# VectorE branches right behind the selection; diagonals and slot numbers behind the first rows' copy; six small loads on ScalarE's queue

## The chip, the cores and the metric

The kernel runs on one core of a Trainium2 chip. The metric is the device time of one execution in microseconds (us): the median of 3 runs of the kernel before is 1742.47 us (1740.42 to 1742.9).

## The reference, cut to what matters

The program is a small network of 256 tokens of width 1024, in float32: a pooling mixer, a mixture of experts (layer 0), latent attention, a mixture of experts (layer 1), and then a second block (state space scan, linear attention, cross attention, feed-forward). The change touches both mixtures of experts, and in them only the routing and the start of the loop over the experts:

```python
def hier_moe(h, rg_w, rg_b, re_w, re_b, w_gate, w_up, w_down):
    gp = softmax(ht @ rg_w + rg_b)                 # 4 groups: top 1
    el = (ht @ re_w + re_b) of the chosen group    # 8 experts: top 2
    gates = g_prob[:, None] * top_p / top_p.sum(-1, keepdims=True)
    expert_ids = g_idx[:, None] * 8 + top_i        # 32 experts, 256 x 2 assignments
    # assignments are sorted by expert, every expert does
    y = (silu(xr @ w_gate[e]) * (xr @ w_up[e])) @ w_down[e]
    # and row y is added to its token, times its gate
```

## The kernel before, in words

Every engine has one program in order of its instructions; semaphores order them against each other. SyncE's queue (SP) loads nearly all weights as slabs of 2 MB into a ring of six places; one further slab per layer goes to a place of its own in the arena (`load_ahead`). A slab may be loaded when the one that held its place is done, which TensorE (PE) tells by `slabs_done`. Each of the 32 experts has three slabs: w_gate, w_up, w_down.

At the start of a mixture of experts PE computes the router's logits, VectorE (DVE) the top group, the top two experts of each token, the number of tokens of each expert (`cnt`), their running sum (`incl`) and from them the sorted position of each assignment (`pos`). The first position of each expert and the largest count go to `starts` (L1868, L1869, semaphore `route_done`). DVE then writes the selection matrix `sel` in two halves (L1875 to L1884). PE sorts the tokens with it (`sort`, L804): `sort(0)` fills the first half of the sorted rows in PSUM; DVE (`sorted_out`, L1904, k tiles 0 to 3) and ScalarE (ACT, L1481, k tiles 4 to 7) copy it to `xs` in SBUF. PE has a piece of the cross attention's keys behind `sort(0)` (L941 to L944).

Behind the selection DVE before writes eight diagonal tiles (L1886 to L1890: positions and gates as diagonals, from which PE's L823 makes rows by a matmul with ones) and the slot numbers of the gates (L1891 to L1896, and in layer 0 a reciprocal for another stage, L1899, for which GpSimd, POOL, waits). Then each of DVE, ACT and PE reads the largest count into a register (L1978, L1543, L946) and branches (L1980, L1545, L948) to one of two bodies, with one window of 64 rows per expert or with four. On this data it is the one with one window, `experts(1)`. 

DVE's body loads two start positions into registers (L1964), copies half 0 out of PSUM, waits until ACT has too, and copies the rows of the first expert and then of the second into two window buffers (`window`, L1925, copy L1933). PE's first matmuls of the experts (`gate_up`, L847, matmul L863) wait for the first window. After `gate_up` of expert 0 PE does the first `beside` (L817): the diagonals' matmul (L823, waits for the second `select_ready`) and half of `sort(1)`; then `gate_up` of expert 1, the other half of `sort(1)`, and then `turn_hid` of expert 0 (L873, transposes L879). This one waits for `hidden`, which needs ACT's `silus` (L1490, L1496) and DVE's product (L1940), and for `slots_ready`, DVE's copy of the diagonals' rows (L1943), which stands behind that product.

SP, in layer 0, waits behind the seven slabs that fit ahead of the experts for `route_max`, and then issues the four router loads of layer 1 (`router_loads`, L531 to L534) and the two halves of `b_in` (L547), all of small pieces; behind them stands the slab that takes the first place that comes free (L574). ACT issues its own transfers on its own queue, among them `kx_park` (L1446), and in `experts` of layer 0 runs on to `silus` of expert 0 right behind it (L1531, L1539).

Of the kernel before, what the change touches and what calls it, by code (L numbers as in the profile page):

```python
# [21 lines left out]
ALU = mybir.AluOpType  # L22
# [3 lines left out]
P = 128  # L26
T = 256
TT = T // P
# [23 lines left out]
TOP_K = 2  # L52
# [264 lines left out]
def program(nc, a, out):  # L317
    with ExitStack() as ctx:
# [24 lines left out]
        def cc(name):  # L343
            at, n = CONST_COLS[name]
            return const[:, at:at + n]
# [161 lines left out]
        gain2 = ar(7680, D)  # L507

        block = ctx.enter_context(nc.Block())


        @block.sync
        def _(sp):
# [15 lines left out]

            def router_loads(layer):  # L530
                sp.dma_start(rw[:, :, 0:GROUPS], a["router_group_w"][layer].rearrange("(k p) g -> p k g", p=P)).then_inc(s["row_loaded"], 16)  # L531
                sp.dma_start(rw[:, :, GROUPS:], a["router_expert_w"][layer].rearrange("(k p) g -> p k g", p=P)).then_inc(s["row_loaded"], 16)
                sp.dma_start(rb[:, 0:GROUPS], a["router_group_b"][layer].partition_broadcast(P)).then_inc(s["row_loaded"], 16)
                sp.dma_start(rb[:, GROUPS:], a["router_expert_b"][layer].partition_broadcast(P)).then_inc(s["row_loaded"], 16)  # L534

            sp.dma_start(memt, a["mem_2"].rearrange("b (t p) d -> p (b t) d", p=P)).then_inc(s["mem_loaded"], 16)
            router_loads(0)

            sp.wait_ge(s["vec2_loaded"], 16 * (len(VEC_PARTS) - FIRST_VECTORS))
            sp.wait_ge(s["pool_loaded"], 16 * 3)  # L540

            def loads_ahead():

                sp.wait_ge(s["route_max"], 1)
                router_loads(1)
                for ri, n in enumerate(("re", "im")):
                    sp.dma_start(b_in[:, ri], a[f"s5_b_{n}_2"][0].rearrange("(j g) p h -> (g p) j h", g=2)).then_inc(s["s5_loaded"], 16)  # L547

# [13 lines left out]
            def experts(layer, n0):  # L562
# [30 lines left out]
                if layer == 0:  # L593
                    load_ahead()
                    loads_ahead()
                for j in range(first + 1, 2 * RING):
# [792 lines left out]
        def _(act):  # L1389
# [61 lines left out]
            def moe(layer, name, n0):  # L1451
# [35 lines left out]
                def experts(windows):  # L1487
# [38 lines left out]
                    if layer == 0:  # L1526
                        act.wait_ge(s["xkv_mm"], 1)
                        park_keys(0, 2, 7)
                        act.wait_ge(s["slabs_done"], n0)
                        act.activation(xk_out[0][:, 2, :], PS[:, 6, 0:T], ACT.Copy).then_inc(s["xkv_out"], 1)  # L1530
                        store_keys(0, 3, 2)  # L1531
                    else:
                        act.wait_ge(s["slabs_done"], n0)
                        act.activation(xk_out[5][:, 1:3, :].rearrange("p f n -> p (f n)"), PS[:, 7, :], ACT.Copy).then_inc(s["xkv_out"], 1)
                        store_keys(5, 3, 10)
# [215 lines left out]
        def _(dve):  # L1751
# [55 lines left out]
            def moe(layer, name, n0):  # L1807
# [77 lines left out]

                for i, v in enumerate((pos, gat)):  # L1886
                    for k in range(TOP_K):
                        for t in range(TT):
                            last = dve.tensor_scalar(diag[:, i, k * TT + t, :], ident, v[:, k, t, :], None, ALU.mult)
                last.then_inc(s["select_ready"], 1)  # L1890
                for w in range(WINDOWS):  # L1891
                    dve.tensor_scalar(slot_of[:, w, :], incl, cc("row_1")[:, w:w + 1], None, ALU.add)
                    last = dve.tensor_scalar(slot_valid[:, w, :], cnt, cc("row")[:, w:w + 1], None, ALU.is_gt)
                step(last)
                step(dve.tensor_tensor(slot_of, slot_of, slot_valid, ALU.mult))
                step(dve.tensor_scalar(slot_of, slot_of, 1.0, None, ALU.subtract))  # L1896
                if layer == 0:
                    dve.wait_ge(s["s5_th"], 2)
                    dve.reciprocal(den, den).then_inc(s["s5_small"], 1)  # L1899
                dve.wait_ge(s["fgain_loaded"], 16)  # L1900
# [12 lines left out]

                dve.wait_ge(s["route_done"], q + 1)

                def experts(windows):
# [8 lines left out]
                    def window(e, w, start=None):  # L1925

                        if isinstance(e[0], int) and linear(e, windows, w) == 2:
                            sorted_wait(1)
                        if isinstance(e[0], int) and linear(e, 1, 0) >= EXPERTS:
                            return  # L1930
                        if start is None:
                            start = load_start(e)
                        dve.tensor_copy(xw[(e[1] * windows + w) % 2], xs[:, :, bass.ds(start + w * WINDOW, WINDOW)])\  # L1933
                           .then_inc(g["window"], 1)

# [27 lines left out]

                    second = after((0, 0), 0)  # L1964
                    start_0, start_1 = load_start((0, 0)), load_start(second[0])
                    sorted_out(0)
                    dve.wait_ge(s["pad_ready"], q + 1)
                    sorted_wait(0)
                    window((0, 0), 0, start_0)
                    window(*second, start_1)  # L1970
                    for w in range(windows):
# [528 lines left out]
```

## Time and profile before

| | us |
|---|---|
| median of 3 runs | 1742.47 (1740.42 to 1742.9) |
| the profiled execution, as timed | 1745.04 |
| its span in the trace | 1743.2 |
| PE busy in the span | 1630.2 (94%) |
| DVE busy | 451.9 (26%) |
| ACT busy | 232.0 (13%) |
| weights on SP's queue | 502.05 MB, 71.9% of 16 engines' span |

Times in the trace count from the start of the span. "Busy" of an engine leaves out registers, branches, semaphores and the issue of DMAs; these appear under an engine's name with a q (DVEq, ACTq, SPq), the duration of a DMA's line being what its issue took, not the transfer. In square brackets stands how long the engine sat idle before a line, and what released it. "x64" counts records; a float32 matmul has two. "PEclk" is the granted share of TensorE's 2.4 GHz clock (1.00 is 2.4 GHz, 0.50 is 1.2 GHz). "DMA share" is the mean busy share of the 16 DMA engines.

### The profile page before, as it was taken

The numbers are of one execution on the slowest core, as the hardware profiler recorded it, in microseconds if no ns is written. First come the engines' busy times: TensorE is split into PE (matmuls) and PEld (weight loads), VectorE is DVE, ScalarE is ACT, GpSimd is POOL, SyncE is SP. The second block draws the span as 40 slices with busy tenths as digits, with TensorE's granted clock in tenths as the row PEclk, the third lists the DMA queues.
The fourth block names the chain that finished last, engine by engine and source line by source line (L and its number), as shares of the span: only waits on it lengthen the run. The fifth ranks groups of instructions, "written<-read, shape, count | busy, mean of one in ns | idle before, by whom it ended". The sixth has DMA issues, their size and how long they took to land.

```text
span 1743.2 us, 22328 instructions
## 1 busy us (share of the span) xinstructions
PE 1630.2 (94%) x9157; PEld 1014.8 (58%) x9157; DVE 451.9 (26%) x967; ACT 232.0 (13%) x503; POOL 97.5 (6%) x165
## 2 busy tenths in 40 slices
PE   7999988888899999999988888889999998999998
PEld 7755444444446657655444444448577777688843
DVE  4211111111113324221111111134976211244411
ACT  4110100000002121111000000021123012100000
POOL 2200000000000000193000000010000000000000
PEclk9999999999999999999999999998999999999999
DMA  9999999999997342899999999995233541444400
GB/s 334 350 378 426 427 427 425 426 425 426 426 413 279 136 169 98 318 417 425 427 425 426 427 427 427 425 376 204 102 140 111 184 134 60 131 163 153 145 24 24
DMA packets 106755, 508.21 MB, mean 292 GB/s; under 512 B 16874, under 2 KB 46155, under 8 KB 73675
## 3 DMA queue, kind: packets, MB, share of 16 engines
q1 hardware_dynamic: 104411, 502.05, 71.9%
q10 hardware_dynamic: 2288, 5.40, 0.8%
q8 instruction: 37, 0.61, 0.1%
q14 instruction: 19, 0.16, 0.0%
HBM read 504.28 MB, written 3.15 MB: 291 GB/s over the span
## 4 chain that ended last, share of the span: by engine, by line
PE 39%; DMA 16%; DVE 3%; ACT 1%; issue 1%; DVEq 0%; ACTq 0%
DMA ring<-in_w_up 16%; PE PS L1355 9%; PE PS L863 6%; PE PS L1120 5%; PE PS L1365 4%; PE PS L1131 2%; PE PS L906 2%; PE PS L1294 2%; PE PS L1304 2%; PE PS L1283 2%; PE PS L892 1%; ACT XN L1412 1%; PE PS L808 0%; DVE arena L2122 0%; PE PS L1332 0%
## 5 line engine op out<-in xcount | busy, mean ns | idle before, releaser
L863 PE MATMUL PS<-ring,arena 128*64 128x256 f32 x4032 | 461.0, 383 | 69.3 <-DMA ring<-in_w_up 51.5
L863 PEld LDWEIGHTS PS<-ring,arena 128*64 128x64 f32 x4032 | 290.9, 137 | 260.5 <-DMA ring<-in_w_up 71.1
L906 PE MATMUL PS<-ring,arena 128*64 128x512 f32 x1024 | 233.8, 598 | 1.2 <-ACT arena L1504 1.2
L1940 DVE TENSOR_TENSOR arena<-PS,arena 128x256 f32<-128x256 f32 x64 | 27.2, 425 | 737.8 <-ACT arena L1496 737.8
L906 PEld LDWEIGHTS PS<-ring,arena 128*64 128x64 f32 x1024 | 68.2, 136 | 157.9 <-issue 157.9
L1355 PE MATMUL PS<-hT,ring 128*128 128x256 f32 x704 | 152.2, 379 | 0.6 <-issue 0.6
L1355 PEld LDWEIGHTS PS<-hT,ring 128*128 128x128 f32 x704 | 133.7, 190 | 18.9 <-issue 0.8
L892 PE MATMUL PS<-arena,hT 64*128 64x512 f32 x512 | 127.2, 615 | 1.9 <-ACT arena L1513 1.9
L1120 PE MATMUL PS<-hT,ring 128*128 128x256 f32 x448 | 101.1, 387 | 1.0 <-issue 1.0
L1120 PEld LDWEIGHTS PS<-hT,ring 128*128 128x128 f32 x448 | 86.6, 195 | 14.8 <-issue 2.8
L1504 ACT ACTIVATE arena<-PS 128x256 f32<-128x256 f32 x64 | 24.6, 384 | 519.3 <-PE PS L879 519.3
L1513 ACT ACTIVATE arena<-PS 128x512 f32<-128x512 f32 x64 | 38.2, 597 | 306.2 <-PE PS L906 306.2
L1365 PE MATMUL PS<-ring,arena 128*128 128x512 f32 x176 | 75.7, 592 | 0.0
L892 PEld LDWEIGHTS PS<-arena,hT 64*128 64x128 f32 x512 | 44.0, 186 | 41.5 <-issue 30.2
L1365 PEld LDWEIGHTS PS<-ring,arena 128*128 128x128 f32 x176 | 33.4, 190 | 41.7 <-issue 41.4
L1952 DVE SCALAR_TENSOR_TENSOR hT<-hT,arena 128x512 f32<-128x512 f32 x64 | 51.4, 803 | 0.2
L2117 DVE TENSOR_SCALAR arena<-PS,VT 128x256 f32<-128x256 f32 x52 | 24.9, 537 | 93.7 <-PE PS L1355 93.2
L2122 DVE SCALAR_TENSOR_TENSOR arena<-PS,VT,arena 128x255 f32<-128x255 f32 (+2 forms) x112 | 46.8, 475 | 1.2
L1412 ACT ACTIVATE XN<-X 128x1024 f32<-128x1024 f32 x18 | 18.9, 1050 | 174.7 <-DVE X L2296 72.7
L728 PE MATMUL PS<-const 128*128 128x128 f32 x222 | 29.1, 287 | 6.7 <-DMA const<-in_const 6.7
L1933 DVE COPY arena<-arena 128x512 f32 x64 | 28.2, 443 | 26.5 <-issue 23.0
L879 PEld LDWEIGHTS PS<-const,arena 128*128 128x128 f32 x128 | 20.3, 206 | 24.8 <-issue 24.7
(387 smaller groups left out, 1390.7 us busy)
## 6 DMA issues: line engine op xcount, KB each, us to landing
ring<-in_w_up SPq DMA_DIRECT2D x64, 2048.0 KB, 25.6
ring<-in_w_down SPq DMA_DIRECT2D x64, 2048.0 KB, 24.6
ring<-in_w_gate SPq DMA_DIRECT2D x62, 2048.0 KB, 25.5
ring<-in_f_w_up SPq DMA_DIRECT2D x22, 1024.0 KB, 6.6
ring<-in_w_in SPq DMA_DIRECT2D x9, 2048.0 KB, 13.2
ring<-in_f_w_down SPq DMA_DIRECT2D x5, 2048.0 KB, 7.9
arena<-in_w_gate SPq DMA_DIRECT2D x2, 2048.0 KB, 22.4
ring<-in_x_wkv SPq DMA_DIRECT2D x2, 2048.0 KB, 8.0
```

What stands on the lines that cost most here:

```text
L863: mm = pe.matmul(PS[half * WINDOW:(half + 1) * WINDOW, bank, m * half_f:(m + 1) * half_f], xw[bank][:, k, :], mat[:, k, half * half_f:(hal ...
L892: mm = pe.matmul(PS[:, 4 + 2 * t + half, :], buf[rows, t * P:(t + 1) * P], y2[rows, :], start=first, stop=last, skip_group_check=True)
L906: mm = pe.matmul(PS[half * WINDOW:(half + 1) * WINDOW, 3, :], hidT[:, w, k * WINDOW:(k + 1) * WINDOW], mat[:, k, half * 512:(half + 1) * 5 ...
L1120: mm = pe.matmul(PS[:, b, f % 2 * T:(f % 2 + 1) * T], w[:, k, f * P:(f + 1) * P], x[:, k, :], start=(k == 0), stop=(k == kx - 1))
L1131: mm = pe.matmul(PS[:, bank + t, :], x[:, k, t * P:(t + 1) * P], w[:, k, :], start=(k == 0), stop=(k == kx - 1))
L1283: mm = pe.matmul(PS[:, 2 * half + t, :], hT[:, k, t * P:(t + 1) * P], w[:, k, :], start=(k == 0), stop=(k == KD - 1))
L1355: mm = pe.matmul(PS[:, 2 * (j % 2) + h, f * T:(f + 1) * T], w[:, k, h, f * P:(f + 1) * P], hT[:, k, :], start=(k == 0), stop=(k == KD - 1))
L1365: mm = pe.matmul(PS[:, 4 + 2 * t + half, :], gF[:, c, t * P:(t + 1) * P], w[:, c - 4 * j, half * 512:(half + 1) * 512], start=(c == 0), st ...
L1412: act.activation(XN[:, t, :], src[:, t, :], ACT.Square, accum_out=ssq[:, t:t + 1]).then_inc(s["norm_ssq"], 1)
L1513: act.activation(y2, PS[:, 3, :], ACT.Copy).then_inc(g["y_sbuf"], 1)
L1952: dve.scalar_tensor_tensor(gates2, slots[:, 0, :], slot_of[:, w, bass.ds(linear(e, 1, 0), 1)], slots[:, 1, :], ALU.is_equal, ALU.mult).the ...
L2122: ins = dve.scalar_tensor_tensor(v, ps(f)[:, 0:T - back], taps[f][back], v, ALU.mult, ALU.add)
```

## The change

Three edits. (1) On DVE, the diagonals and the slot numbers are made into two functions (`spread`, `window_slots`), and called inside both bodies behind the branch: the first window's copy, `spread`, the second window's copy, `window_slots`. (2) The first window's start is the constant 0 and not a register; the second's is loaded where its window is copied. (3) SP no longer waits for `route_max` nor issues the router loads of layer 1 and `b_in`; ACT issues these six, in layer 0, behind `kx_park`'s store and before `silus` of expert 0.

```diff
--- before.py
+++ after.py
@@ -506,6 +506,12 @@
         cacc = [ar(5632 + 1024 * i, 4, T) for i in range(2)]
         gain2 = ar(7680, D)
 
+        def router_loads(eng, layer):
+            eng.dma_start(rw[:, :, 0:GROUPS], a["router_group_w"][layer].rearrange("(k p) g -> p k g", p=P)).then_inc(s["row_loaded"], 16)
+            eng.dma_start(rw[:, :, GROUPS:], a["router_expert_w"][layer].rearrange("(k p) g -> p k g", p=P)).then_inc(s["row_loaded"], 16)
+            eng.dma_start(rb[:, 0:GROUPS], a["router_group_b"][layer].partition_broadcast(P)).then_inc(s["row_loaded"], 16)
+            eng.dma_start(rb[:, GROUPS:], a["router_expert_b"][layer].partition_broadcast(P)).then_inc(s["row_loaded"], 16)
+
         block = ctx.enter_context(nc.Block())
 
 
@@ -527,24 +533,11 @@
                 sp.dma_start(s5_rows[at:at + S5J, :], a[name][0].rearrange("(j g) p -> j (g p)", g=2)).then_inc(s["s5_loaded"], 16)
             sp.dma_start(ldt2[32:32 + S5J, :], a["s5_log_dt_2"][0].rearrange("(j g) -> j g", g=2)).then_inc(s["s5_loaded"], 16)
 
-            def router_loads(layer):
-                sp.dma_start(rw[:, :, 0:GROUPS], a["router_group_w"][layer].rearrange("(k p) g -> p k g", p=P)).then_inc(s["row_loaded"], 16)
-                sp.dma_start(rw[:, :, GROUPS:], a["router_expert_w"][layer].rearrange("(k p) g -> p k g", p=P)).then_inc(s["row_loaded"], 16)
-                sp.dma_start(rb[:, 0:GROUPS], a["router_group_b"][layer].partition_broadcast(P)).then_inc(s["row_loaded"], 16)
-                sp.dma_start(rb[:, GROUPS:], a["router_expert_b"][layer].partition_broadcast(P)).then_inc(s["row_loaded"], 16)
-
             sp.dma_start(memt, a["mem_2"].rearrange("b (t p) d -> p (b t) d", p=P)).then_inc(s["mem_loaded"], 16)
-            router_loads(0)
+            router_loads(sp, 0)
 
             sp.wait_ge(s["vec2_loaded"], 16 * (len(VEC_PARTS) - FIRST_VECTORS))
             sp.wait_ge(s["pool_loaded"], 16 * 3)
-
-            def loads_ahead():
-
-                sp.wait_ge(s["route_max"], 1)
-                router_loads(1)
-                for ri, n in enumerate(("re", "im")):
-                    sp.dma_start(b_in[:, ri], a[f"s5_b_{n}_2"][0].rearrange("(j g) p h -> (g p) j h", g=2)).then_inc(s["s5_loaded"], 16)
 
             def place_free(n):
                 m = held_before(n)
@@ -592,7 +585,6 @@
                     placed(j)
                 if layer == 0:
                     load_ahead()
-                    loads_ahead()
                 for j in range(first + 1, 2 * RING):
                     placed(j)
                 turns = EXPERT_SLABS // RING
@@ -1529,6 +1521,11 @@
                         act.wait_ge(s["slabs_done"], n0)
                         act.activation(xk_out[0][:, 2, :], PS[:, 6, 0:T], ACT.Copy).then_inc(s["xkv_out"], 1)
                         store_keys(0, 3, 2)
+                        act.wait_ge(s["logits"], 1)
+                        act.wait_ge(s["route_max"], 1)
+                        router_loads(act, 1)
+                        for ri, n in enumerate(("re", "im")):
+                            act.dma_start(b_in[:, ri], a[f"s5_b_{n}_2"][0].rearrange("(j g) p h -> (g p) j h", g=2)).then_inc(s["s5_loaded"], 16)
                     else:
                         act.wait_ge(s["slabs_done"], n0)
                         act.activation(xk_out[5][:, 1:3, :].rearrange("p f n -> p (f n)"), PS[:, 7, :], ACT.Copy).then_inc(s["xkv_out"], 1)
@@ -1883,20 +1880,27 @@
                     if half == 0:
                         last.then_inc(s["select_ready"], 1)
 
-                for i, v in enumerate((pos, gat)):
-                    for k in range(TOP_K):
-                        for t in range(TT):
-                            last = dve.tensor_scalar(diag[:, i, k * TT + t, :], ident, v[:, k, t, :], None, ALU.mult)
-                last.then_inc(s["select_ready"], 1)
-                for w in range(WINDOWS):
-                    dve.tensor_scalar(slot_of[:, w, :], incl, cc("row_1")[:, w:w + 1], None, ALU.add)
-                    last = dve.tensor_scalar(slot_valid[:, w, :], cnt, cc("row")[:, w:w + 1], None, ALU.is_gt)
-                step(last)
-                step(dve.tensor_tensor(slot_of, slot_of, slot_valid, ALU.mult))
-                step(dve.tensor_scalar(slot_of, slot_of, 1.0, None, ALU.subtract))
-                if layer == 0:
-                    dve.wait_ge(s["s5_th"], 2)
-                    dve.reciprocal(den, den).then_inc(s["s5_small"], 1)
+                def spread():
+
+                    for i, v in enumerate((pos, gat)):
+                        for k in range(TOP_K):
+                            for t in range(TT):
+                                last = dve.tensor_scalar(diag[:, i, k * TT + t, :], ident, v[:, k, t, :], None, ALU.mult)
+                    last.then_inc(s["select_ready"], 1)
+
+                def window_slots(step):
+
+                    for w in range(WINDOWS):
+                        dve.tensor_scalar(slot_of[:, w, :], incl, cc("row_1")[:, w:w + 1], None, ALU.add)
+                        last = dve.tensor_scalar(slot_valid[:, w, :], cnt, cc("row")[:, w:w + 1], None, ALU.is_gt)
+                    step(last)
+                    step(dve.tensor_tensor(slot_of, slot_of, slot_valid, ALU.mult))
+                    step(dve.tensor_scalar(slot_of, slot_of, 1.0, None, ALU.subtract))
+                    if layer == 0:
+                        dve.wait_ge(s["s5_th"], 2)
+                        dve.reciprocal(den, den).then_inc(s["s5_small"], 1)
+
+                at_branch = steps[0]
                 dve.wait_ge(s["fgain_loaded"], 16)
                 if layer:
                     dve.wait_ge(s["xkv_stored1"], 16 * 2)
@@ -1912,6 +1916,8 @@
                     dve.wait_ge(s["sorted_act"], KD // 2 * (2 * q + half + 1))
 
                 dve.wait_ge(s["route_done"], q + 1)
+
+                step_dve = step
 
                 def experts(windows):
                     g = loop[layer]
@@ -1930,8 +1936,11 @@
                             return
                         if start is None:
                             start = load_start(e)
-                        dve.tensor_copy(xw[(e[1] * windows + w) % 2], xs[:, :, bass.ds(start + w * WINDOW, WINDOW)])\
-                           .then_inc(g["window"], 1)
+                        if isinstance(start, int):
+                            rows = slice(start + w * WINDOW, start + (w + 1) * WINDOW)
+                        else:
+                            rows = bass.ds(start + w * WINDOW, WINDOW)
+                        dve.tensor_copy(xw[(e[1] * windows + w) % 2], xs[:, :, rows]).then_inc(g["window"], 1)
 
                     def hids(e, w):
                         dve.wait_ge(g["silu"], linear(e, windows, w + 1))
@@ -1961,13 +1970,17 @@
                                 window(*after(next_expert(e), w))
                             window_gates(e, w)
 
-                    second = after((0, 0), 0)
-                    start_0, start_1 = load_start((0, 0)), load_start(second[0])
+                    steps[0] = at_branch
                     sorted_out(0)
                     dve.wait_ge(s["pad_ready"], q + 1)
                     sorted_wait(0)
-                    window((0, 0), 0, start_0)
-                    window(*second, start_1)
+                    window((0, 0), 0, 0)
+                    spread()
+                    if windows == 1:
+                        window((0, 1), 0)
+                    else:
+                        window((0, 0), 1, 0)
+                    window_slots(step_dve)
                     for w in range(windows):
                         hids((0, 0), w)
                         if w:
```

## Rows read from the trace of the kernel before

**Rows 1.** Timeline of PE, layer 0, start of the experts: start, duration, us.

```profile
53.56 4.48 PE L706 MATMUL PS<-arena,ring 128*128 128x256 f32 x20
60.86 8.81 PE L863 MATMUL PS<-ring,arena 128*64 128x256 f32 x64 [2.82 <-DVE arena L1933]
...
75.30 7.13 PE L863 MATMUL PS<-ring,arena 128*64 128x256 f32 x64
...
86.41 0.39 PE L879 MATMUL PS<-const,arena 128*128 128x128 f32 x2
```

**Rows 2.** Timeline of PE, layer 1, the same place.

```profile
700.13 8.58 PE L863 MATMUL PS<-ring,arena 128*64 128x256 f32 x64 [3.67 <-DVE arena L1933]
```

**Rows 3.** Stretches: us, PE, PEld, DVE, ACT, POOL, PEclk, DMA share, GB/s.

```profile
61.40:64.80 3.40, 3.40 (x20) 2.38 (x18) 0.00 (x0) 0.00 (x0) 0.11 (x1) 0.50 0.78 81
...
1450.00:1460.00 10.00, 6.88 (x40) 5.91 (x39) 6.45 (x8) 3.10 (x9) 0.00 (x0) 1.00 0.37 120
```

**Rows 4.** Stretches in layer 0's loop over the experts, columns as above.

```profile
90.00:100.00 10.00, 10.00 (x80) 6.71 (x76) 1.90 (x5) 1.25 (x3) 0.00 (x0) 1.00 0.78 284
...
120.00:130.00 10.00, 10.00 (x66) 4.78 (x64) 1.93 (x4) 1.01 (x3) 0.00 (x0) 1.00 1.00 423
```

**Rows 5.** Timeline of DVE, layer 0, and L1907 of layer 1 last.

```profile
46.93 1.65 DVE L1889 TENSOR_SCALAR arena<-const,arena 128x128 f32<-128x128 f32 x8
...
58.33 1.66 DVE L1907 TENSOR_SCALAR arena<-PS,ffn_gain 128x256 f32<-128x256 f32 x4 [7.70 <-issue]
60.18 0.78 DVE L1933 COPY arena<-arena 128x512 f32 x2 [0.19 <-issue]
...
71.62 1.23 DVE L1943 COPY hT<-PS 128x1024 f32<-128x1024 f32 x1 [1.07 <-PE PS L823]
...
697.60 1.66 DVE L1907 TENSOR_SCALAR arena<-PS,ffn_gain 128x256 f32<-128x256 f32 x4 [4.95 <-issue]
```

**Rows 6.** DVE's branch and the register loads behind it: layer 0, then layer 1.

```profile
L1980 DVEq COMPARE_BRANCH  x1: 90/90/90, 51.4 to 51.4; - x1
L1923 DVEq TENSOR_LOAD <-starts x2: 310/314/319, 57.0 to 57.7; - x2
...
L1980 DVEq COMPARE_BRANCH  x1: 86/86/86, 693.4 to 693.4; - x1
L1923 DVEq TENSOR_LOAD <-starts x2: 304/312/320, 696.3 to 697.0; - x2
```

**Rows 7.** Timeline of ACT: layer 0, and its last sorted copy of layer 1.

```profile
53.76 0.84 ACT L1484 ACTIVATE arena<-PS,ffn_gain 128x256 f32<-128x256 f32 x2 [1.08 <-PE PS L808]
...
58.49 0.35 ACTq L1446 DMA_DIRECT2D kx_park<-arena  x1
58.88 1.28 ACT L1496 ACT_TABLE_LOAD   x1 [0.42 <-ACT arena L1530]
69.71 0.38 ACT L1496 ACTIVATE arena<-PS 128x256 f32<-128x256 f32 x1 [9.55 <-PE PS L863]
...
696.07 0.84 ACT L1484 ACTIVATE arena<-PS,ffn_gain 128x256 f32<-128x256 f32 x2 [1.08 <-PE PS L808]
```

**Rows 8.** Timeline of SP: start of an issue, what it took.

```profile
38.45 17.59 SPq L532 DMA_DIRECT2D arena<-in_router_expert_w  x1
56.08 3.36 SPq L533 DMA_DIRECT2D arena<-in_router_group_b  x1
...
60.73 2.00 SPq L547 DMA_DIRECT2D arena<-in_s_b_im  x1
```

**Rows 9.** DMA view of 639 to 642: packets, MB (q1 SP, q10 ACT).

```profile
q1 hardware_dynamic: 84, 1.11, 87.3%
q10 hardware_dynamic: 84, 0.17, 14.7%
```

**Rows 10.** DMA view, us to landing (last): issued at 58.49, then at 697.42.

```profile
kx_park<-arena ACTq DMA_DIRECT2D x1, 384.0 KB, 3.8
...
kx_park<-arena ACTq DMA_DIRECT2D x1, 384.0 KB, 9.8
```

## The prediction

> **What bounds the kernel now.** I read the stretches first, then the timelines of PE, DVE, ACT and SP at the start of both loops over the experts, and last the DMA view. The stretches show which resource limits each part of such a loop [rows 4]: at 90 to 100 us PE is busy throughout and the DMA engines only 0.78, from 120 on they are at 1.00. SP loads a slab when PE has freed its place, so until the DMA engines are full PE's pace sets everything, and later the weight stream only goes on from where PE let it start. A microsecond won or lost by PE before about 100 us (and at the same place of layer 1, whose loop is the same) is therefore a microsecond at the end, in either direction. In PE's timelines there is one hole before the experts in each layer: 2.82 us at 58.04, where L706 ends, and 3.67 us at 696.46 [rows 1, 2], both ended by DVE's first window copy. Behind the hole the clock is granted at 0.50, the 1.2 GHz level, for 3.4 us [rows 3]: the first `gate_up` takes 8.81 and 8.58 us where the second takes 7.13 [rows 1, 2], 1.68 and 1.45 us more.
>
> **The branch earlier (both layers).** DVE is late because its branch stands behind the diagonals and slot numbers. Before the branch go 8 diagonals, 10 slot instructions and the reciprocal: from 46.93 to 50.62, 3.7 us [rows 5]. From the branch at 51.4 the body's first instruction follows at 57.0 (5.6 us) in layer 0 and 2.9 us later in layer 1, where few weights stream [rows 6]. The two register loads take 1.3 us more (57.0 to 58.33) [rows 5, 6]; the first goes (constant 0), the second moves to the second window, about 0.6 us behind `spread`.
>
> Layer 1: the branch comes at about 689.7, the body at 692.6, `sorted_out` ends near 694.4. Next late is ACT: its last sorted copy ends at 696.91 [rows 7]. With the 0.19 us between, one copy (0.43) and 0.24 to PE, PE starts at 697.7 and not at 700.13: 2.4 us won. The hole is then 1.3 us. Holes like it leave the clock at 1.00: a stretch with 3.1 us of PE idle within 10 keeps it [rows 3]. So I add 1.5 us: 3.9 us. ACT covers 2.6 us of a slower branch, so even layer 0's 5.6 us would cost nothing here. Bounds: 0 (PE's own code, for which no row gives a time free of DVE, is late too) and 3.67 + 1.45 = 5.1 us.
>
> Layer 0: branch at 47.7, body at 53.3 (still under the weights, so 5.6 us), `sorted_out` done at 55.0, ACT at 54.6 [rows 7], window at 55.7: before PE's end of L706 at 58.04. PE then waits for its own branch only. Bounds for its start are 58.1 and 60.8; I take 59.3, the middle. That alone would be worth 1.5 us and, with the smaller hole, the 1.7 us of clock: 3.2 us (0 to 4.4).
>
> `spread` (1.65 us) and `window_slots` (about 2.0 us) behind the first window are free: the first is wanted at the end of `gate_up`, 7 us later, the second behind `hids`; without that cover they cost 3.7 us per layer. POOL gets its reciprocal some 10 us later; nothing behind it is wanted before layer 1. The removed issues on SP let w_up go at 58.1 instead of 62.77: worth 0, since the DMA engines run empty again at 90 to 100 [rows 4], all slabs landed.
>
> **The six loads on ACT (layer 0).** They stand in ACT's program between `kx_park`'s issue (58.49 to 58.84) and the table load and SiLU of expert 0; the wait for `logits` and `route_max` is over by then. Queued behind them are SiLU (at 69.71 before), thereby DVE's product and slot copy, thereby PE's `turn_hid` at 86.41 [rows 1, 7]. So the issue time counts. By the code these are 1024 + 1024 + 128 + 128 + 2048 + 2048 = 6400 pieces of 16 to 128 bytes, 400 for each of 16 engines. The trace has them only on SP: L532's issue took 17.59 us with weights ahead of it in the queue, and once these had drained, from L533's start to the end of b_im's issue, 56.08 to 62.73, 6.65 us passed [rows 8]. An issue holds its engine until earlier small pieces are through.
>
> After the change ACT's pieces go beside SP's weights. Where both queues have work their packets come one for one, 84 and 84 [rows 9], whatever their size (1.11 against 0.17 MB); the same `kx_park` store, 8 pieces per engine, lands in 3.8 us beside small pieces, in 9.8 us beside weights [rows 10]. A slab at 423 GB/s [rows 4] takes 5.0 us, 0.6 us for each of 8 pieces per engine (16 of half the size for w_down). ACT's queue thus moves some 8 to 16 pieces per engine and slab, while the first two loads have 128, and L533 was let in only when they were nearly through.
>
> When do the weights pause? w_up goes at 58.1; with PE from 59.3, w_down at 62.9 and w_gate at 66.4 follow without a gap: a stream of 15 us plus the store until 74.8. By then 32 pieces per engine have passed, 8 of them against the store: 24 of 128 gone. The second `gate_up` starts at 72.1 (12.8 us behind the first at full clock, [rows 1]) and frees places at 75.7 and 79.2: a pause of 1 to 2 us, then weights until 86.4. The remaining 104 of 128 want 81% of L533's 3.36 us, 2.7 us: not done in the pause. PE meanwhile arrives at `turn_hid` at 59.3 + 23.9 = 83.2 (86.41 - 60.86 - 1.68) and stands. From 86.4 no weights are left: 0.7 us for the rest, 59.44 to 62.73 = 3.3 us for the other four, and ACT is free near 90 (88 if the pause does suffice, 93 if it is used for nothing). Table load 1.28, SiLU to product 0.42, product 0.42, slot copy 1.23, 0.1 to PE [rows 5, 7]: `turn_hid` at 93.5, 7.1 us later than before. A hole of 10 us lowers the clock for certain: 1.7 us more [rows 3]. Layer 0's 3.2 us are gone with it, being waited away.
>
> The Trainium skill says something else here. "DMA: Bandwidth & Descriptors", section "Queues, rings and completion order", has an engine take turns between queues by whole packets, typically 9 to 17 descriptors from one queue before it switches. By that rule the first 128 pieces would need some ten turns, ACT would be free near 73, and the sum would be the gain alone. The same page, section "Issuing engines are not separate DMA queues", says that a second issuing engine saves only issue time; that is against the edit too.
>
> **Sum.** Layer 0: +7.1 + 1.7 = +8.8 us; layer 1: -3.9 us; together +4.9 us. The profiled execution took 1745.04 us (span 1743.2 and 1.84 around it), 2.6 above the median, about what one or two clock dips are worth; the sum is a difference, so it goes onto the median: 1742.47 + 4.9 = 1747.4 us. With ACT free at 88 or 93 it is 1745.4 or 1750.4.
>
> **Rivals.**
> (a) The hold stays within the cover. PE stands only if ACT is free later than 83.2 - 3.5 = 79.7 us. Either ACT's pieces go in bundles per turn, or its queue takes all six without holding it. Then layer 0 gives 3.2 and layer 1 3.9: 1742.47 - 7.1 = 1735.4 us (1734 to 1739). For it: ACT's own issues took 0.35 us each [rows 7]. Against: those were of 8 pieces per engine, and rows 9 and 10 speak for turns of one. 30 in 100, of them 13 for the bundles.
> (b) The early branch doesn't help: PE's own code arrives no sooner than it starts now, so layer 1 gives nothing, beside the hold: +8.8, 1751.3 us. For it: DVE's branch takes 2.9 to 5.6 us, PE's is as late in layer 0 (it can only branch behind `sort`). Against: in layer 1 PE has 3.67 us for it and is released 0.24 us after DVE's copy [rows 2]. 10 in 100.
> (c) The hold ends between 80 and 86, the pause being longer than reckoned (PE at 60.1 lengthens it by 0.8): 1738 to 1744. 5 in 100.
>
> **How the numbers follow.** The forecast, ACT's hold beyond the cover with layer 1's gain, has 55 in 100, and its own range is 1744 to 1751. A measurement of this kernel can tell about 0.2%, 3.5 us. Of the forecast's 55, 37 are over 1746, 17 within, 1 below 1739; (a) is 29 faster, 1 within; (b) slower; (c) 2 faster and 3 within. That gives 32 faster and 21 within and 47 slower. The range for 8 in 10 takes in most of (a): 1734.5 to 1751.5.
>
> **What would show it.** DVE's branch near 47.7 and 689.7; PE's first L863 near 59.3 and 697.7 with PEclk 1.00 behind it; in ACT's queue the load of `router_group_b` or `b_im` with an issue of over 10 us; SiLU of expert 0 near 91 instead of 69.71; a PE hole of about 10 us before L879, put down to DVE's L1943 or L1940. Wrong it is if ACT's issues together take under 20 us, if SiLU comes before 81, or if there is no hole before L879.

## The result: 0.3% slower, and the profile after

The kernel after takes 1749.92 us (median of 7 runs, 1745.26 to 1753.65; the profiled execution 1751.8, its span 1750.0); the kernel before, run beside it, 1742.9 us. The ratio is 1.0031 (95% interval 1.0019 to 1.0044), which is +5.4 us, 3.3 to 7.7. A second set on another occasion (e11 below) gave 1.0024 (1.0014 to 1.0033). The forecast was 1747.4 us. Below, a hole is a stretch in which PE stands idle, and ACT's hold is the time for which its own issues keep it from its next work.

Lines of the kernel after are numbered some 8 lower than before on PE and ACT: L855 is `gate_up` (before L863), L871 the transposes of `turn_hid` (L879), L898 `down` (L906), L1488 SiLU (L1496), L1943 the window's copy (L1933). All times of layer 0 are some 3.7 us later than before, since in this execution the clock was at 0.50 already from 37 to 44 us; e11 does not show that, so it is no part of the change. The timeline of PE, first layer 0, then layer 1, against [rows 1, 2]:

```profile
57.27 4.48 PE L698 MATMUL PS<-arena,ring 128*128 128x256 f32 x20
61.69 7.13 PE L855 MATMUL PS<-ring,arena 128*64 128x256 f32 x64
...
95.95 0.70 PE L871 MATMUL PS<-const,arena 128*128 128x128 f32 x2 [10.24 <-DVE hT L1952]
97.27 5.99 PE L898 MATMUL PS<-ring,arena 128*64 128x512 f32 x16 [0.62 <-ACT arena L1496]
103.08 3.63 PE L855 MATMUL PS<-arena 128*64 128x256 f32 x32
...
708.35 7.13 PE L855 MATMUL PS<-ring,arena 128*64 128x256 f32 x64 [1.34 <-DVE arena L1943]
```

The hole ahead of the first `gate_up` is gone in layer 0 and 1.34 us instead of 3.67 in layer 1, and both run at full clock, 7.13 us. In its place stands a new hole of 10.24 us ahead of `turn_hid`, with `down` at half clock behind it (5.99 us where it takes 3.65). The third `gate_up` starts 41.3 us behind the end of the keys' matmuls (103.08 - 61.75); before it was 32.8 (90.88 - 58.04). DVE's timeline, layer 0, against [rows 5]:

```profile
56.40 1.66 DVE L1911 TENSOR_SCALAR arena<-PS,ffn_gain 128x256 f32<-128x256 f32 x4 [5.67 <-PE PS L800]
58.44 0.43 DVE L1943 COPY arena<-arena 128x512 f32<-128x512 f32 x1 [0.39 <-ACT arena L1476]
```

DVE, before the last to arrive, now waits itself, for PE's `sort` and then for ACT's copy. The timelines of ACT and its queue, then of SP, against [rows 7, 8]:

```profile
62.20 0.35 ACTq L1438 DMA_DIRECT2D kx_park<-arena  x1
...
63.08 3.79 ACTq L511 DMA_DIRECT2D arena<-in_router_expert_w  x1
66.89 6.18 ACTq L512 DMA_DIRECT2D arena<-in_router_group_b  x1
73.11 7.45 ACTq L513 DMA_DIRECT2D arena<-in_router_expert_b  x1
80.59 1.26 ACTq L1528 DMA_DIRECT2D arena<-in_s_b_re  x1
81.88 10.72 ACTq L1528 DMA_DIRECT2D arena<-in_s_b_im  x1
...
93.92 0.38 ACT L1488 ACTIVATE arena<-PS 128x256 f32<-128x256 f32 x1
...
61.79 0.33 SPq L567 DMA_DIRECT2D ring<-in_w_up  x1
65.40 0.38 SPq L567 DMA_DIRECT2D ring<-in_w_down  x1
```

ACT is in its own six issues for 29.9 us (62.66 to 92.60) and gives SiLU at 93.92, though its input was there at 68.8. The DMA view counts packets by queue (q1 SP, q10 ACT); here for 66 to 69, 72 to 74 and 79 to 82 us, against [rows 9]:

```profile
q1 hardware_dynamic: 64, 1.05, 89.9%
q10 hardware_dynamic: 46, 0.14, 11.5%
...
q1 hardware_dynamic: 100, 0.82, 96.7%
q10 hardware_dynamic: 100, 0.00, 2.9%
...
q1 hardware_dynamic: 58, 0.69, 70.2%
q10 hardware_dynamic: 1909, 0.14, 46.6%
```

At 72 to 74 the queues move 100 packets each, though SP's are of 8 KB and ACT's of a few bytes. Only when the weights pause, at 79 to 82, do 1909 small pieces pass. The stretches behind them (us, PE, PEld, DVE, ACT, POOL, PEclk, DMA share, GB/s), against [rows 4]:

```profile
90.00:100.00 10.00, 3.43 (x10) 1.30 (x12) 3.88 (x8) 3.78 (x8) 0.00 (x0) 0.50 0.41 88
100.00:110.00 10.00, 10.00 (x76) 5.72 (x72) 1.19 (x3) 0.60 (x1) 0.00 (x0) 0.90 0.54 205
```

While PE stands, no place in the ring comes free and the weights stop too (88 and 205 GB/s; before, 284 and 355 in the same stretches). From some 120 us on the DMA share is 1.0, and from 223 us on PE has a gap of 1.1 to 1.2 us in every expert for its weights, so the loop's end hangs on the stream of weights. Of the 8.5 us by which the third `gate_up` is late against the kernel before, 6.9 are left at the loop's end; against e1 below they are 13.1 and 13.2 us, so there nothing is caught up.

### The profile page after: what moved, and what is told of

The parts are those of the page before. It is cut to its first block, busy times and chain, and to the rows that moved or that the text cites. A ratio compares the mean times of both kernels' runs of the same rounds, so it can differ in the third digit from the quotient of the medians.

```text
span 1750.0 us, 22321 instructions
## 1 busy us (share of the span) xinstructions
PE 1634.7 (93%) x9157; PEld 1017.7 (58%) x9157; DVE 451.9 (26%) x967; ACT 231.9 (13%) x503; POOL 97.3 (6%) x165
## 4 chain that ended last, share of the span: by engine, by line
PE 59%; DMA 33%; DVE 4%; ACTq 2%; ACT 1%; issue 1%; SPq 0%; DVEq 0%
DMA ring<-in_w_up 32%; PE PS L855 12%; PE PS L1347 9%; PE PS L1112 5%; PE PS L898 4%; PE PS L1357 4%; PE PS L1123 2%; PE PS L884 2%; PE PS L1286 2%; PE PS L1296 2%; PE PS L1275 2%; PE PS L713 2%; PE PS L1095 2%; PE PS L698 1%; PE PS L800 1%; PE PS L682 1%
## 5 line engine op out<-in xcount | busy, mean ns | idle before, releaser
L855 PE MATMUL PS<-ring,arena 128*64 128x256 f32 x4032 | 457.6, 381 | 62.8 <-DMA ring<-in_w_up 50.4
L855 PEld LDWEIGHTS PS<-ring,arena 128*64 128x64 f32 x4032 | 288.6, 137 | 252.8 <-DMA ring<-in_w_up 69.5
L898 PE MATMUL PS<-ring,arena 128*64 128x512 f32 x1024 | 236.2, 603 | 1.2 <-ACT arena L1496 1.2
L1949 DVE TENSOR_TENSOR arena<-PS,arena 128x256 f32<-128x256 f32 x64 | 27.2, 425 | 743.1 <-ACT arena L1488 743.1
L898 PEld LDWEIGHTS PS<-ring,arena 128*64 128x64 f32 x1024 | 68.8, 138 | 159.9 <-issue 159.9
L1496 ACT ACTIVATE arena<-PS 128x256 f32<-128x256 f32 x64 | 24.6, 384 | 503.4 <-PE PS L871 503.4
L871 PE MATMUL PS<-const,arena 128*128 128x128 f32 x128 | 32.4, 335 | 10.2 <-DVE hT L1952 10.2
L871 PEld LDWEIGHTS PS<-const,arena 128*128 128x128 f32 x128 | 20.3, 207 | 35.3 <-issue 24.7
L720 PE MATMUL PS<-const 128*128 128x128 f32 x222 | 30.9, 298 | 7.1 <-DMA const<-in_const 7.1
```

Of the source, the lines that this page charges most:

```text
L855: mm = pe.matmul(PS[half * WINDOW:(half + 1) * WINDOW, bank, m * half_f:(m + 1) * half_f], xw[bank][:, k, :], mat[:, k, half * half_f:(hal ...
L871: mm = pe.transpose(PS[:, 2, c * P:(c + 1) * P], hid_rows[:, c, :], ident)
L898: mm = pe.matmul(PS[half * WINDOW:(half + 1) * WINDOW, 3, :], hidT[:, w, k * WINDOW:(k + 1) * WINDOW], mat[:, k, half * 512:(half + 1) * 5 ...
```

## The experiments

All were timed beside the kernel before. The table has the ratio to it, the same in us (of 1743.5), and from the profiles the loop over the experts: from the end of the keys' matmuls to the last `down`, in layers 0 and 1.

| kernel | median | ratio (95%) | us | layer 0 | layer 1 |
|---|---|---|---|---|---|
| before | 1743.5 | 1 | 0 | 466.2 | 465.3 |
| after | 1749.9 | 1.0031 (1.0019-1.0044) | +5.4 | 473.1 | 461.5 |
| e1 | 1734.2 | 0.9944 (0.9929-0.9958) | -9.8 | 459.9 | 461.3 |
| e2 | 1743.0 | 0.9997 (0.9981-1.0013) | -0.5 | 462.5 | 465.2 |
| e3 | 1737.4 | 0.9962 (0.9945-0.9978) | -6.6 | 462.5 | 461.0 |
| e4 | 1741.0 | 0.9986 (0.9975-0.9997) | -2.4 | 462.7 | 467.9 |
| e5 | 1734.3 | 0.9948 (0.9932-0.9964) | -9.1 | 459.8 | 462.5 |
| e7 | 1740.5 | 0.9983 (0.9973-0.9993) | -3.0 | 461.2 | 465.1 |
| e8 | 1743.0 | 1.0003 (0.9989-1.0016) | +0.5 | 465.5 | 461.8 |
| e9 | 1737.2 | 0.9966 (0.9954-0.9978) | -5.9 | 462.0 | 461.7 |
| e10 | 1745.6 | 0.9999 (0.9981-1.0017) | -0.2 | 471.1 | 461.7 |
| e11 | 1747.1 | 1.0024 (1.0014-1.0033) | +4.2 | 471.9 | 461.6 |

The fillers of e4, e8 and e10 stand behind the keys' matmuls and are in these figures. The medians of before beside the experiments were 1743.3 to 1743.9 us.

**e1, loads back on SP.** The kernel after without its third edit (in short).

```diff
-   act: router_loads(act, 1); two loads of b_in      # behind kx_park
+   sp:  wait route_max; router_loads(sp, 1); two loads of b_in   # behind load_ahead()
```

> The kernel after, with the six small loads back on SyncE's queue in their old place; the earlier branch stays. My theory (the loss is ACT held by its own DMA issues, the early branch is a gain in both layers): PE's first gate_up of layer 0 follows the keys' matmuls with no hole at full clock (-2.8 -1.7 us), layer 1 keeps -3.8 us, turn_hid is released by ACT and DVE as early as before; together about -8.3 us against the kernel before, 1734.6 us, ratio 0.995. Rival A (part of the loss comes from the early branch itself or from w_up let in sooner): no more than -4 us, ratio 0.998 or above. Rival B (the spread behind the first window's copy delays turn_hid): a hole of some us ahead of turn_hid also here.

With e5 it is the fastest kernel, 9.8 us (7.3 to 12.4) ahead of the kernel before. PE's timeline, layer 0 and layer 1:

```profile
59.06 7.13 PE L859 MATMUL PS<-ring,arena 128*64 128x256 f32 x64
...
82.93 0.39 PE L875 MATMUL PS<-const,arena 128*128 128x128 f32 x2
...
690.86 7.13 PE L859 MATMUL PS<-ring,arena 128*64 128x256 f32 x64 [1.25 <-DVE arena L1942]
```

No hole in layer 0, neither ahead of `gate_up` nor of `turn_hid`; both rivals fall. PE's own branch adds nothing: its compare (L944) starts at 56.0 us, 3.1 us ahead of the keys' end, while earlier matmuls still run. The third `gate_up` follows 28.3 us behind the keys (87.40 - 59.13), 4.6 us earlier than before, and 2.82 + 1.68 explain 4.5 of them.

**e2, the loads on ACT alone.** The kernel before with its branch as it was (in short).

```diff
-   sp:  wait route_max; router_loads(1); two loads of b_in
+   act: wait logits, route_max; router_loads(1, act); two loads of b_in   # behind kx_park
```

> The kernel before with edit 3 alone: the six small loads on ScalarE's queue, the branch where it was. My theory: ACT's issues take about 30 us in all, SiLU of expert 0 comes near 90 instead of 69.7, turn_hid 28 to 34 us behind its place at the keys' end becomes 34 us, i.e. some 6 us later than before plus 1.7 to 3.6 us of half clock behind the hole; layer 1 unchanged: +8 to +11 us, ratio about 1.005 to 1.006. With e1 it should add up to the whole change: e1 (-8.3) + e2 - 2.8 -1.7 of gain waited away. Rival (the loads are hidden once PE starts later by its hole): 0 to +2 us, ratio within 1.001.

My theory fell: 0 and not +8 to +11 us, though the edit is the same. ACT's queue, SP's and PE:

```profile
60.08 3.84 ACTq L511 DMA_DIRECT2D arena<-in_router_expert_w  x1
63.95 4.81 ACTq L512 DMA_DIRECT2D arena<-in_router_group_b  x1
68.79 0.46 ACTq L513 DMA_DIRECT2D arena<-in_router_expert_b  x1
...
71.87 8.39 ACTq L1528 DMA_DIRECT2D arena<-in_s_b_im  x1
...
81.59 0.38 ACT L1488 ACTIVATE arena<-PS 128x256 f32<-128x256 f32 x1
...
58.80 0.33 SPq L567 DMA_DIRECT2D ring<-in_w_up  x1
65.16 0.38 SPq L567 DMA_DIRECT2D ring<-in_w_down  x1
...
61.45 7.13 PE L855 MATMUL PS<-ring,arena 128*64 128x256 f32 x64 [2.69 <-DVE arena L1930]
...
85.31 0.39 PE L871 MATMUL PS<-const,arena 128*128 128x128 f32 x2
```

The issues took 20.6 us here, SiLU came at 81.59, and the hole ahead of `turn_hid` didn't arise. `router_expert_b` took 0.46 us to issue where it took 7.45. What differs is PE's late start: w_down comes 6.36 us behind w_up and not 3.61. The DMA view of 66 to 69 us:

```profile
q10 hardware_dynamic: 2115, 0.39, 70.9%
q1 hardware_dynamic: 65, 0.43, 38.8%
```

ACT's first two loads, 2048 pieces, passed in a pause between w_up and w_down, which the kernel after lacks (46 of q10 in its stretch of 66 to 69, and then one for one). So the theory was amended: **with w_up let in at the keys' end, PE's hole made the pause in which the small pieces pass; closing the one closes the other.** The runs from e5 on test this; e3 bears on it too. The 12 times of e2 reach from 1738.9 to 1754.3, the five of e1 from 1733.1 to 1735.6; only one execution of each has a profile.

**e3, no weights beside the loads.**

```diff
    load_ahead()
+   sp.wait_ge(s["s5_loaded"], 16 * 5)     # until b_in, the last of ACT's loads, has landed
```

> The kernel after, but SyncE issues no further weights until ACT's six loads have landed. Theory (ACT is held because its small pieces take turns one for one with the pieces of the weights): without weights beside them the six issues take some 7 us together instead of 30, SiLU of expert 0 comes at about 71 us, no hole ahead of turn_hid; the weights held back for some 7 us have their cover (the DMA engines ran empty at 90 to 100 us): about -8 us against the kernel before, 1734 to 1736 us. Rival (a DMA of many small pieces is slow to issue on ScalarE whatever runs beside it): issues stay near 30 us, total +5 to +7 us. Second rival (the weights are needed): a wait for slabs in PE later in layer 0 gives some us back.

ACT's six issues take 5.8 us; the last of them, and the first weights behind them:

```profile
63.11 2.18 ACTq L1529 DMA_DIRECT2D arena<-in_s_b_im  x1
...
68.12 0.33 SPq L567 DMA_DIRECT2D ring<-in_w_up  x1
```

So the weights beside them hold the issues, not ACT or their number. The time is 3.3 us above e1 by the medians, and layer 0 2.6 us longer (462.5 against 459.9), with no hole in its first three experts: PE's gaps for weights begin at 190 us (those of over 1 us at 194) instead of 207. Weights held back till 68 are not free, as the second rival had it; by the timed runs alone the difference from e1 is within the two intervals.

**e5, only the router's loads on ACT.** The four router loads stay on ACT, `b_in` goes back to SP.

> The kernel after with the four router loads still on ACT but the two halves of b_in back on SyncE's queue. My first theory (ACT's loads cost +8 to +11 us wherever PE's hole is) fell with e2: there the hold was 21.1 us and SiLU came at 81.59, in time for turn_hid at 85.31. New theory: the hold ends with pauses in the stream of weights; with 144 small pieces per engine and not 400, ACT is free in the first pause, at the latest 18.9 us behind the keys' end as the router loads were in the kernel after (61.75 to 80.59), SiLU 1.3 us later, turn_hid not delayed: total near e1, about -9 us, ratio 0.995. Rival (any small load on ACT beside the weights costs in proportion to its pieces, 144/400 of 15.8 us): -3.5 us, ratio 0.998.

As fast as e1. But ACT's four issues took 2.8 us in all (59.79 to 62.55), not up to 19: SP was itself in `b_in` until 60.22, and its weights began behind that. The rival (a cost by the piece) falls; the pause was not tested, since no weights ran beside the loads.

**e7, a smaller dose of the early branch.** The kernel before, `spread` alone moved behind the first window's copy.

> The kernel before with one part of the early branch alone: only the eight diagonals stand behind the first window's copy (the slot numbers and both register loads stay ahead, the loads stay on SyncE). Theory (VectorE's time ahead of the first window adds one for one to PE's hole until the hole is used up): hole 2.82 - 1.65 = 1.2 us in layer 0 and 3.67 - 1.65 = 2.0 us in layer 1, clock kept: -3.3 -1.7 -1.45 = -6.4 us at the most, -3.3 us if the clock still falls; ratio 0.996 to 0.998. Rival (the branch costs what it costs, only the loads count): within 1 us of the kernel before.

```profile
60.91 7.13 PE L863 MATMUL PS<-ring,arena 128*64 128x256 f32 x64 [1.26 <-DVE arena L1936]
...
695.10 8.81 PE L863 MATMUL PS<-ring,arena 128*64 128x256 f32 x64 [2.05 <-DVE arena L1936]
```

The holes shrink by 1.56 and 1.62 us, the 1.65 us of the diagonals, one for one. The clock held in layer 0 and fell in layer 1. By that -4.6 us were due (1.56 + 1.68 + 1.62 - 0.23); the timed runs gave -3.0 (-4.7 to -1.2).

**e4, the hole filled.** The kernel before with ten matmuls of no use ahead of PE's wait.

```diff
+   keep_busy(4, 10)
    pe.wait_ge(s["route_done"], q + 1)
```

> The kernel before, with ten idle matmuls on a free PSUM bank put ahead of PE's wait in the hole before the first gate_up, in both layers; their results are used by nobody. Theory (the half clock in the first 3.4 us of gate_up is there because PE stood idle for 2.8 and 3.7 us ahead of it): first gate_up takes 7.13 us instead of 8.81 and 8.58, total -3.1 us, 1739.4 us, ratio 0.998. Rival (the dip has another cause, or moves elsewhere): durations stay at 8.6 to 8.8 us or a dip shows up at another place, 0 us.

```profile
62.74 7.13 PE L863 MATMUL PS<-ring,arena 128*64 128x256 f32 x64 [0.49 <-DVE arena L1934]
...
698.30 1.91 PE L863 MATMUL PS<-ring,arena 128*64 128x256 f32 x14 [1.29 <-DVE arena L1934]
702.36 7.51 PE L863 MATMUL PS<-ring,arena 128*64 128x256 f32 x50 [2.14 <-issue]
```

-2.4 us (-4.4 to -0.5). In layer 0 the clock holds. The profiled execution is the slowest of its eleven (1748.12 us): in layer 1 a new hole of 2.14 us stands inside `gate_up`, for which the profile shows no releaser, and the clock fell behind it all the same (7.51 us for the last 50 records); layer 1 is 2.6 us longer. Whether the other executions had this hole stays open. And e2's layer 0 kept full clock behind 2.69 us of hole where the kernel before lost it behind 2.82: a hole of this size lowers the clock in some executions only. Whether the filler or chance kept it in e4's layer 0 is thus not shown.

**e8, a filler in the kernel after.** 24 matmuls of no use put where the hole was, in layer 0.

```diff
+   if layer == 0:
+       keep_busy(4, 24)
    pe.wait_ge(s["route_done"], q + 1)
```

> The kernel after with 24 matmuls of no use (2.6 us at full clock, results used by nobody) ahead of PE's first gate_up in layer 0, where the kernel before has its hole. New theory (PE's hole made SyncE issue w_down and what follows 2.7 us later against w_up; that is the pause in which ACT's first 128 pieces per engine pass; the early branch closed the hole and with it the pause): more useless work makes it faster: ACT's six issues take about 21 us in all instead of 30, no 10 us hole ahead of turn_hid, -10 -2.3 +2.6, about -10 us against the kernel after, i.e. -4 to -6 us against the kernel before, ratio 0.997. Rival (the hold does not hang on PE's start): +2.6 us on top of the kernel after, ratio 1.005 or more.

```profile
58.10 5.52 PE L720 MATMUL PS<-const 128*128 128x128 f32 x48
63.55 7.13 PE L855 MATMUL PS<-ring,arena 128*64 128x256 f32 x64
...
87.41 0.39 PE L871 MATMUL PS<-const,arena 128*128 128x128 f32 x2
...
68.19 0.46 ACTq L513 DMA_DIRECT2D arena<-in_router_expert_b  x1
```

The filler took 5.5 us, twice what I had reckoned, and yet the kernel is 4.9 us faster than the kernel after by ratios (6.9 by medians; 3.7 by ratios against e11). The issues take 22.3 us, the hole ahead of `turn_hid` is gone. w_down came 8.97 us behind w_up, and the pause was there: 2211 packets of q10 passed from 64 to 70 us. In this profile work of no use on PE stopped the weights for a moment, and with that the hole went. Against the kernel before I had expected -4 to -6 us and measured +0.5 (-1.9 to 2.8); with 5.5 us of filler in my sum in place of 2.6 it gives -1.4, inside the interval. The profiled execution (1739.06 us) is the second fastest of the 12, so whether the slower ones had the pause stays open.

**e9, a pause made directly.** PE untouched; SP holds w_down until ACT's four router loads have landed.

```diff
    for j in range(first + 1, 2 * RING):
+       if layer == 0 and j == first + 2:
+           sp.wait_ge(s["row_loaded"], 64 * 2)
        placed(j)
```

> The kernel after, but in layer 0 SyncE lets w_up go and holds the next slab (w_down) until ACT's four router loads have landed, and nothing later: one pause of some 3 us put into the stream of weights, PE untouched. New theory: ACT's six issues end within 15 us behind kx_park's store, SiLU well ahead of turn_hid; weights 3 to 5 us late in the stream have partly the cover of the later pauses: total -6 to -9 us against the kernel before, between e3 (-5.9) and e1 (-9.2). Rival (a pause must be as long as all the small pieces, as in e3): a hold of 20 us or more and a hole ahead of turn_hid.

```profile
59.22 0.33 SPq L567 DMA_DIRECT2D ring<-in_w_up  x1
72.56 0.38 SPq L567 DMA_DIRECT2D ring<-in_w_down  x1
...
73.65 0.38 ACT L1490 ACTIVATE arena<-PS 128x256 f32<-128x256 f32 x1
...
82.98 0.39 PE L873 MATMUL PS<-const,arena 128*128 128x128 f32 x2
```

-5.9 us (-8.0 to -3.8), at the edge of the -6 to -9 expected, the issues 12.3 us, no hole. One pause suffices, and with PE's program unchanged it is the timing of the weights, not work on PE, that frees ACT; its price, as in e3, is in the weights (layer 0 2.1 us longer than e1).

**e10, half the filler.** As e8 with `keep_busy(4, 12)`.

> The kernel after with 12 matmuls of no use ahead of PE's first gate_up in layer 0, half of the last filler; as 24 of them took 5.5 us, these take 2.75 us, the size of the hole in the kernel before. Theory (the pause between w_up and w_down sets how many of ACT's pieces pass; w_up's data took about 7 us, so a pause needs w_down to be let in over 5 us behind w_up): w_down comes 6.4 us behind w_up as in e2, the pause is about 2 us, ACT's issues take 21 to 23 us, SiLU less than 2 us ahead of where it would delay turn_hid: about 2.7 us faster than the last filler, 1740 us, ratio 0.998. Rival (the hold shrinks with the filler in proportion): half of the shortening seen with 24, some 26 us of issues, a hole of 4 to 6 us ahead of turn_hid and about 1745 us.

```profile
69.01 7.45 ACTq L513 DMA_DIRECT2D arena<-in_router_expert_b  x1
...
90.41 0.70 PE L871 MATMUL PS<-const,arena 128*128 128x128 f32 x2 [4.78 <-DVE hT L1954]
```

and the DMA view of its 66 to 69 us:

```profile
q10 hardware_dynamic: 1906, 0.38, 64.0%
q1 hardware_dynamic: 65, 0.52, 44.0%
```

I expected what e2 shows, and the profile shows what the rival said: issues of 27.2 us and a hole of 4.78 us, though w_down came 6.30 us behind w_up, nearly as in e2. The packets speak for this reason: 1906 packets of q10 passed, where e2 had 2115. `kx_park`'s 8 pieces on each engine and the 128 of the first two loads make 2176 in all. A pause nearly long enough left a few pieces behind, and `router_expert_b` waited 7.45 us for them, till 76.46, while the weights went on (q1's share is 84 to 118% in every us from 69 to 78). From 70 to 72 q10 moved 12 packets a us to q1's 50; at one for one that is about a quarter of the engines (an estimate) that still had small pieces. The sum over all engines alone does not tell when an issue is let in: here it was not with 1943 packets through, in the kernel after it was with 1830, and there `router_group_b` with 232. The rule behind that stays open. The 12 times, 1736.1 to 1739.3 (3 runs) and 1742.9 to 1750.0 (9 runs), are a hint of all or nothing rather than the rival's proportion; only one of these executions has a profile.

**e11, the kernel after again.**

> The kernel after, unchanged, beside the half filler on the same chip: ratio 1.003 to 1.004 and a hole of 10 us ahead of turn_hid again, if the loss belongs to the kernel and not to one chip or one execution; the profile also shows whether the half clock before the sort (37 to 44 us in the first profile) comes again.

```profile
92.96 0.70 PE L871 MATMUL PS<-const,arena 128*128 128x128 f32 x2 [9.76 <-DVE hT L1952]
```

The hole is 9.76 us, the issues 29.5 us; the ratio, 1.0024, is a little under the expected. The half clock at 37 to 44 us is absent.

## Why the prediction was right, and where it was not

- **The early branch, layer 1** (forecast -3.9 us): hole 3.67 to 1.34, `gate_up` 8.58 to 7.13, together -3.78; ACT's last sorted copy is next, as named. The loop of layer 1 is 3.8 us shorter in the kernel after, and 461.0 to 462.5 us in all eight kernels with the whole early branch against 465.1 to 467.9 in the four without it.
- **The early branch, layer 0** (forecast -3.2): undersized. PE started 0 us behind the keys and not 1.3; I had taken the middle between the bounds, and the lower one was right. By e1 this part is worth -4.5 us.
- **`spread` and `window_slots` free:** holds; DVE has them done at 62.8, 6 us ahead of the end of the first `gate_up`.
- **w_up earlier on SP, worth 0:** not tested by itself. With PE on time it is worth nothing: e5 and e1 let w_up in 1.4 and 4.2 us behind the keys' end, and their loops take 459.8 and 459.9 us. With PE late there is a hint of 1.8 us: from the third `gate_up` to the loop's end layer 0 takes 433.3 us in the kernel before and 431.5 in e2, which lets w_up in 4.7 us sooner. What the edit did besides is what mattered: it opened the stretch between w_up and w_down that PE's start ends. e3 and e9 show the other direction: weights let in late cost 2 to 3 us.
- **ACT's hold** (forecast: free near 90 with PE's start at 59.3, 32 us behind the keys' end at 58.04): measured 30.9 (92.60 - 61.75). Hole forecast about 10 us, measured 10.24. The working, a stream of 15 us without a gap that lets few pieces in, then a pause, is what the packets show, except that the first pause did suffice for the first 128 pieces, and it was `b_im` that waited for the second.
- **Layer 0's sum** (forecast +8.8): the third `gate_up` is 8.5 us later against the keys' end. Two misses offset each other here, which is luck: `turn_hid` came 5.8 us later than before and not 7.1 (34.2 us behind the keys' end against 28.4), and what follows cost 2.7 us and not 1.7, with 2.3 us of half clock in `down` alone. The hole of 10 us came out right in the same way, PE and ACT both being 1.1 to 1.3 us earlier than forecast.
- **The whole** (forecast +4.9, measured +5.4 and +4.2): the two loops of the profiles account for +3.1 us (6.9 - 3.8) in the kernel after and +2.0 in e11; what makes the rest is not shown.
- **Turns one for one:** 100 to 100 packets (72 to 74 us) and 77 to 76 (76 to 79 us), whatever the size, and in single stretches of 0.2 us still 13 to 13, 10 to 11 and 9 to 8 (72.2 to 72.8 us). The Trainium skill, "DMA: Bandwidth & Descriptors", section "Queues, rings and completion order", has turns of typically 9 to 17 descriptors. This trace does not agree: in 0.2 us an engine does less than one packet of the weights, and turns of that size would make such counts uneven. The rival of 1735.4 us, though, did not follow from that rule, which holds for both queues: with turns of that size on either side the pieces would still pass one for one on average, and ACT would not have been free near 73. What the Trainium skill says on the same page, section "Issuing engines are not separate DMA queues", that a second issuing engine saves only issue time, agrees: the move saved SP's and cost ACT's, and e5, with four of the loads on ACT, is no faster than e1.
- **The clock behind small holes:** full behind 1.34 and 1.25 us, as forecast. The ground given for it was weak: the 3.1 us of idle time in [rows 3] are two holes of 2.01 and 1.11 us (L979, L1332), and behind one of 2.05 us the clock fell in e7.
- **Where the reasoning was thin:** I priced the two edits as separate terms and counted layer 0's 3.2 us as waited away. The runs show that they are not separate: e1 alone -9.8, the loads alone -0.5, together +5.4 and +4.2. Some 15 us arise only from both (15.7 by the first set, 14.5 by e11). The term "+7.1" is thus no price of the loads, but of the loads beside a stream whose pause the other edit had closed. Rival (c) had the direction (PE later, pause longer) and too small a size.

## What to carry to other kernels

A DMA of many small pieces can hold the engine that issues it at its next issue until most of those pieces have passed, and beside a stream of large pieces, with turns one for one, that was mostly until the stream's next pause: ask first where the pauses are and who makes them. A hole on the busiest engine can be what makes such a pause; when a hole is closed, look at what lived in it. Test the two halves of a change apart before pricing them apart: here the half with the gain alone (e1) was 15 us faster than the whole kernel after.

## What I had not expected of the hardware

- PE's branch did not show: the first `gate_up` follows the keys' matmuls directly in e1, and in e8, where PE's compare (L942) starts at 62.3 us, only 1.3 us ahead of `gate_up`, there is no hole either. DVE's took 5.6 and 2.9 us [rows 6] and in layer 1 of the kernel after again 2.8 (702.61 - 699.8).
- How little it takes to miss a pause: in e10's stretch of 66 to 69 us the DMA view has 1836 packets under 512 B, so some 212 of 2048 pieces were left over, and the issue behind them took 7.45 us instead of 0.46.
- The stretches at half clock differ between executions of one kernel: over the whole program 24 us in the profile of e1, 42 in those of before and e11, 56 in the first of after. Some of that is the change's: without the stretches at the start of the experts it is 24 us in e1, 35 in before, 32 in e11 and 42 in after. Not all of a difference between two profiles is therefore the change's; compare stage by stage. From the third `gate_up` to the loop's end, layer 0 takes 431.5 to 431.9 us in eight of the 12 profiles, layer 1 between 431.4 and 433.0.
